# Overflow test at the end of each engine's expert program, and a later semaphore clear, in a two-layer trunk on one Trainium2 core

## What is computed

```python
gates = jnp.einsum('tk,tke->te', wts, jax.nn.one_hot(expert_id, N_EXPERTS, dtype=f32))
hg = jnp.einsum('td,edf->tef', t, w_gate)
hu = jnp.einsum('td,edf->tef', t, w_up)
hid = jax.nn.silu(hg) * hu * gates[:, :, None].astype(hg.dtype)
out = jnp.einsum('tef,efd->td', hid, w_down)
```

## Time and profile before

| | us |
|---|---|
| median of 3 runs | 1789.06 |
| lowest, highest | 1786.23, 1791.18 |
| profiled execution | 1784.8 |
| its span, first to last instruction | 1783.0 |
| PE busy | 1465.4 (82%) |
| DVE, ACT, POOL busy | 652.1, 460.8, 190.6 |
| mean granted TensorE clock | 0.897 |
| HBM traffic | 228 GB/s over the span |

### The profile page before, as it was taken

How to read it: one execution, slowest core, us unless ns; L and a number is a source line. 1 busy time by engine, 2 the same in 40 slices (tenths; PEclk the granted TensorE clock), 3 DMA queues, 4 the chain that set the end, 5 groups by cost and what they waited for, 6 DMA issues and landing times. The chain is left out here.

```text
span 1783.0 us, 25386 instructions
## 1 busy us (share of the span) xinstructions
PE 1465.4 (82%) x10279; PEld 1078.5 (60%) x10279; DVE 652.1 (37%) x1268; ACT 460.8 (26%) x804; POOL 190.6 (11%) x314
## 2 busy tenths in 40 slices
PE   4999789868889678699489978848999839998865
PEld 2999444455679433499355544448999726554435
DVE  3312165543235575742611111143245541111104
ACT  3222265532124542421301100132124211110012
POOL 0000033210000143000011111020000001111101
PEclk8999899889989787799689999958999869999985
DMA  7232587649921601420989999931223399999954
GB/s 291 71 95 72 217 331 263 233 154 370 351 77 48 244 0 47 154 85 11 380 323 390 383 392 402 372 114 48 87 80 98 115 393 336 387 391 393 395 221 151
DMA packets 133593, 399.73 MB, mean 224 GB/s; under 512 B 15842, under 2 KB 67682, under 8 KB 110690
## 3 DMA queue, kind: packets, MB, share of 16 engines
q1 hardware_dynamic: 114370, 359.01, 53.7%
q10 hardware_dynamic: 11488, 21.24, 3.3%
q0 software_dynamic: 7616, 17.84, 3.2%
HBM read 368.72 MB, written 37.19 MB: 228 GB/s over the span
## 5 line engine op out<-in xcount | busy, mean ns | idle before, releaser
L2871 PE MATMUL ex_gups<-ex_gu,ex_he 128*64 128x256 f32 x1728 | 210.3, 399 | 46.7 <-DMA ex_gu<-in_moe_w_up 43.8
L2871 PEld LDWEIGHTS ex_gups<-ex_gu,ex_he 128*64 128x64 f32 x1728 | 126.3, 143 | 114.8 <-DMA ex_gu<-in_moe_w_up 48.8
L2916 DVE TENSOR_TENSOR ex_hid<-ex_sg,ex_gups 128x128 f32<-128x128 f32 x64 | 18.4, 287 | 298.5 <-ACT ex_sg L2940 298.5
L2889 PE MATMUL ex_yps<-ex_dn,ex_hid_t 128*64 128x512 f32 x512 | 123.9, 604 | 0.9 <-issue 0.9
L2849 POOL DMA_INDIRECT ex_hg<-h_rows,route_tok x64 | 60.2, 941 | 509.1 <-PE ex_trps L2861 425.3
L225 PE MATMUL sc_ps<-h_hi,sc_hi 128*128 128x272 f32 x352 | 101.7, 289 | 0.5 <-PEq L3127 0.5
L225 PE MATMUL sc_ps<-hT_r,sc_hi 128*128 128x272 f32 x352 | 100.9, 287 | 0.0
L225 PE MATMUL sc_ps<-h_hi,sc_w_r 128*128 128x272 f32 x352 | 100.7, 286 | 0.0
L2940 ACT ACTIVATE ex_sg<-ex_gups 128x128 f32<-128x128 f32 x64 | 17.7, 277 | 299.7 <-PE ex_gups L2871 299.7
L2930 ACT ACTIVATE ex_yo<-ex_yps 128x512 f32<-128x512 f32 x64 | 38.2, 597 | 184.9 <-PE ex_yps L2889 184.9
L2909 DVE COPY ex_he<-ex_trps 128x512 f32<-128x512 f32 x64 | 44.2, 691 | 64.6 <-PE ex_trps L2861 64.6
(11 more groups left out here) (535 smaller groups left out, 3382.0 us busy)
## 6 DMA issues: line engine op xcount, KB each, us to landing
ex_dn<-in_moe_w_down SPq DMA_DIRECT2D x64, 1024.0 KB, 26.4
ex_gu<-in_moe_w_gate SPq DMA_DIRECT2D x54, 1024.0 KB, 24.9
ex_gu<-in_moe_w_up SPq DMA_DIRECT2D x54, 1024.0 KB, 26.5
ada_rest_w<-in_ada_w SPq DMA_DIRECT2D x40, 1024.0 KB, 6.4
as_pages<-in_cache_kT SPq DMA_DIRECT2D x32, 512.0 KB, 6.5
as_pages<-in_cache_v SPq DMA_DIRECT2D x32, 512.0 KB, 5.6
y_rows<-ex_yo ACTq DMA_DIRECT2D x128, 128.0 KB, 7.0
qkv_w<-in_mix_w_in SPq DMA_DIRECT2D x12, 1024.0 KB, 5.4
```

What stands on the lines that cost most here:

```text
L2871: last = nc.tensor.matmul(gu_ps[64 * q:64 * q + 64, :, :], he[n % 2][:, j, :], ex.gu[n % S][:, :, j, q * P:(q + 1) * P], start=(j == 0), s ...
L2889: last = nc.tensor.matmul(y_ps[n % 2][64 * c:64 * c + 64, :], hid_t[:, m * CAP:(m + 1) * CAP], ex.dn[n % S][:, m, c * 512:(c + 1) * 512], ...
L2916: nc.vector.tensor_tensor(hid[:, :], sg[:, :], gu_ps[:, 1, :], ALU.mult).then_inc(done["hid"], 1)
```

## The change

It does three things:

1. The overflow pass no longer has a block of its own. Each engine's load of the count, test and overflow program stand at the end of that engine's main program, ahead of the barrier that ends the experts' block.
2. Since no barrier separates the passes any more, the overflow programs of SP, POOL, PE and DVE begin with waits on the main pass's counters. These waits are inside the part that is skipped at a count of zero.
3. `moe` does not clear semaphores at its end. In layer 0 those of routing and experts are cleared with the next clear, behind combining and short convolution. In layer 1 no clear follows.

```diff
             def sync_program(sp):
+                sp.wait_ge(done["y"], NE)
                 for b in range(MORE):
                     load_slot(sp, b, b)
...
             def pool_program(pool):
-
+                pool.wait_ge(done["tr"], NE)
                 for n in range(MORE * rounds):
...
             def tensor_program(pe):
+                pe.wait_ge(done["he"], NE)
+                pe.wait_ge(done["ht"], NE)
+                pe.wait_ge(done["yo"], NE)
                 with pe.Fori(0, rounds) as i:
...
             def vector_program(dve):
+                dve.wait_ge(done["y"], NE)
                 with dve.Fori(0, rounds) as i:
...
         with nc.Block() as block:
+            @block.vector
+            def _(dve):
+
+                for b in range(2):
+                    nc.vector.memset(hg[b][:, :], 0.0).then_inc(rows_clear, 1)
+                vector_main(dve)
+                when_more(dve, more[2])
+
             @block.sync
             def _(sp):
+                sync_main(sp)
                 when_more(sp, more[0])
 
             @block.tensor
             def _(pe):
+                tensor_main(pe)
                 when_more(pe, more[1])
-
-            @block.vector
-            def _(dve):
-                when_more(dve, more[2])
 
             @block.scalar
             def _(act):
+                scalar_main(act)
                 when_more(act, more[3])
 
             @block.gpsimd
             def _(pool):
+                pool_main(pool)
                 when_more(pool, more[4])
...
         phase_route(k, layer, r, ahead)
         phase_experts(k, layer, r, ex, slots)
-    k.recycle()
     return r, slots
```

More of the change, by code:

```diff
@@ L3034, in block_programs @@
             return sync_program, tensor_program, vector_program, scalar_program, pool_program
-        with nc.Block() as block:
-            @block.vector
-            def _(dve):
[L3040 to L3058, removed]
         w_more = [k.sem(f"{nm}w_more{b}") for b in range(MORE)]
```

## The result

| | before | after |
|---|---|---|
| median, us | 1789.32 (13 runs, 1786.23 to 1796.38) | 1780.71 (13 runs, 1774.12 to 1787.82) |
| ratio after/before | | 0.9947, 95% interval 0.9932 to 0.9961 |
| profiled execution, us | 1784.8 | 1777.8 |
| its span, us | 1783.0 | 1776.1 |

The change makes the kernel about 0.5% faster: 9.5 us by the ratio, 8.6 us by the medians. The forecast was 9.8 us less, 1779.3 us, with a range from 1773.5 to 1785.0.

What follows compares the result with a forecast made beforehand. The prediction took control between ACT's last stores and POOL's first combining gather to bound the kernel: 5.2 + 4.9 = 10.1 us saved, less 0.3 for the clear, gives 9.8; 1789.1 - 9.8 = 1779.3 us, range 1773.5 to 1785.0.

Steps and rivals of the forecast that it cites:

- The path and what bounds it: Between ACT's last store wait and POOL's first combining gather: pure control, setting the end one for one; 10.1 us saved together.
- The uncovered test on ACT: End of ACT's expert program: loading and testing the count stays exposed, 0.9 us in layer 0, 0.8 in layer 1.
- PE's jump under cover: End of PE's expert program: the roughly 3.5 us jump hides behind ACT's landing stores, 1.8 and 2.1 us to spare; charge 0.
- The prediction's reading of why only PE pays: PE's jump over 116 matmuls leaves the instruction pages held, forcing a DMA fetch: 3.5 us against 0.05.
- The clear: After layer 0's combining and short convolution: the merged semaphore clear grows from 0.22 us, costing +0.3 us.
- Layer 0's gain arrives: From layer 0's combining into layer 1: nothing swallows the gain, and layer 1's first weight load comes 4.9 us earlier.
- rival 2: Downstream of layer 0: its gain is swallowed by the expert weight stream or clock turns; 1784.5 us, chance 0.06.
- Rival 1: PE's jump twice as long, outlasting its cover (layer 1: through at 1732.4); 1782.5 or 1786.5 us; chance 0.12.
- Rival 3: Short convolution: TensorE's clock comes back later, 0.46 us lost per us at the low level; up to 1795.4 us, chance 0.04.
- The clock during the combining: Start of combining: TensorE at the low level before and after despite PE's shorter wait; no gain counted.
- The base: Starting time for the forecast: the median of three runs, 1789.1 us, rather than the profiled execution's 1784.8 us.

Runs made afterwards that it cites:

- e3: The changed kernel with PE held until ACT's last stores have landed, before its load and test of the count; 1788.0 us, ratio 1.0000 to the kernel before.
- e5: The kernel before with an overflow pass of 2 blocks a round instead of 4 (58 matmuls for PE to skip, not 116); 1785.1 us, ratio 0.9967.
- e6: The changed kernel with an overflow pass of 2 blocks a round instead of 4; 1781.8 us, ratio 0.9956 to the kernel before.
- e8: The changed kernel with ACT's test ahead of its last wait and 2 overflow blocks a round instead of 4; 1779.7 us, ratio 0.9941 to the kernel before.
- e10: The changed kernel with ACT's test ahead of its last wait and the clear back behind both layers' experts; 1779.4 us, ratio 0.9938 to the kernel before.

## Why the prediction was right

**The path and what bounds it.** Right. The gap between ACT's last wait and POOL's gather was pure control on the critical path, and what went from it went from the time: 5.2 and 4.9 us forecast, 5.2 (6.41 to 1.23) and 4.9 us (5.93 to 1.02) measured. The uncovered test on ACT was put at 0.9 and 0.8 us and took 1.0 (load at 1165.9, DRAIN at 1166.9) and 0.8 us.

**PE's jump under cover.** The choice was right, PE's load does not wait for the array: it starts at 1160.2, and the last matmul ends at 1162.1. The cover was to be 1.8 and 2.1 us; it is 1.6 and 1.8, mainly since the jump is 0.5 and 0.3 us longer there. e3 shows that the gain hangs on this cover. The prediction's reading of why only PE pays is confirmed by e5, and by the instruction transfer that every long jump holds and no short one.

**The clear.** Mis-sized: +0.3 us was taken for its growth out of a range up to 0.44. The clear itself went from 0.22 to 0.61 us, +0.39, and the time to the release from 0.6 to 1.1 us, +0.5, because the DRAIN ahead of it is 0.1 us longer too. Net by the gaps 10.1 - 0.5 = 9.6 us, against 9.5 by the ratio.

**Layer 0's gain arrives.** Right, rival 2 is out. Combining and short convolution took 59.1 and 185.2 us (59.0 and 185.4), and layer 1's first expert load, at 1412.9, stands 0.4 us behind the release at 1412.5, as it stood 0.5 behind before. Counted from the start of layer 0's routing that load comes 4.2 us earlier (566.6 and 562.4 us), where the forecast had 4.9: the clear took 0.5 and not 0.3, and the expert pass of this execution was 0.7 us longer:

```profile
L2786 SPq DMA_DIRECT2D ex_gu<-in_moe_w_gate x27: 327/2772/4341, 1412.9 to 1687.3; - x27
```

**Rival 1** was there in effect, a jump 0.3 to 0.5 us longer and not 3.5, and was swallowed by the cover; its cause stays open (e3). Its 1732.4 us is 1732.3 by its own terms, which changes nothing. **Rival 3** did not come: the short convolution's stage is within 0.2 us in every profile (185.2 to 185.4). The clock during the combining was low in both, as said; the combining's own length varies from 58.2 to 59.9 us among the profiles, more than the term that was set to zero.

**The base.** The forecast took the three runs' median, 1789.06, though the profiled execution was 4.3 us lower. With 13 runs the median is 1789.32. The 1.4 us between 1779.3 and 1780.7 are 0.2 us from the clear and for the rest scatter of the medians; the ratio's interval, 0.9932 to 0.9961, holds the forecast's 0.9945.

## What to carry to other kernels

Where stages end in barriers, look for the engine whose last step is only a wait for its own stores: what every other engine has still to do in control (load a count, test, jump) belongs ahead of that barrier, and on that engine itself ahead of its wait. A rare path compiled into the stream can cost even when it is skipped (here 3.5 us for 116 matmuls and 0.35 for 58 on PE, under 0.1 us on the other engines): look at each engine's jump over it, and try a shorter loop body before anything else is rebuilt. Judge such a step by the gap it closes, not by one span; here the spans wandered by 11 us before the first changed instruction.

## What the runs showed of the hardware that was not expected

- PE's jump over 116 matmuls of skipped code takes 3.3 to 3.6 us with PE idle and the DMA engines at 0.02 to 0.03, and 3.7 to 4.3 us straight behind its last matmuls with the DMA engines at 0.51 to 0.62; over 58 it takes 0.35 us in either case (0.35 in e5, 0.33 to 0.35 in e6 and e8). Each long jump holds one instruction transfer of 16 KB, which takes 0.9 to 1.6 us, and ends 1.4 to 1.5 us behind its landing.
- PE's sequencer loads a register from SBUF while matmuls are under way: the load of 1160.2 ran with products going on to 1162.1, in the 0.49 us that it also took with the array at rest.
- After 3.8 us of idle time TensorE was found at the high clock (2.4 GHz) in three executions and at the low one (1.2 GHz) in another, e10.
